# A fourth token tile between two embedding products, a root moved to GpSimd, and PSUM banks counted from 4

## The chip, the cores and the metric

One NeuronCore of a Trainium2 chip runs the whole program as one launch. The metric is the device time in microseconds (us) of an execution; the number given is the median of several runs.

## The reference

The input is x, 512 tokens of 1024 features in float32. The first half of the model has two layers, each a mixer, an MLP and an embedding gate. With LN the layer norm, it reads, cut to what matters here:

```python
for i in range(2):
    y = mixer_i(h)                                   # even: mLSTM + sparse attention; odd: latent attention
    h = _layer_norm(DN_ALPHA * h + y, ln1_g[i], ln1_b[i])
    u = jnp.square(jax.nn.relu(h @ mlp_w1[i])) @ mlp_w2[i]      # 1024 -> 4096 -> 1024
    h = _layer_norm(DN_ALPHA * h + u, ln2_g[i], ln2_b[i])
    h = h + jax.nn.sigmoid(h @ ple_gate_w[i]) * (p[i] @ ple_w[i])
```

The second half has two layers more. Each is a gated ffn, 1024 to 2816 and back, added by half; a hybrid mixer; and a second ffn. In front of each of the three stands a norm, `xf * rsqrt(mean(xf^2) + eps) * g`.

## The kernel before

**Tiles.** X holds the 512 tokens as four token tiles (j or m, 0 to 3) of 128 partitions by 1024 features. A product needs its input with the features on the partitions. So behind each norm TensorE turns every token tile: 8 transposes of 128x128 into two PSUM banks. ScalarE (ACT) copies these rounded ("hi") and VectorE (DVE) writes the difference ("lo") into `H`, which empties the banks. Weights are split the same way: ACT writes a hi half, DVE a lo half, into buffers used in turn. A product is three matmuls, hi*hi, hi*lo and lo*hi.

**Layers.** `lin(name, ...)` is one layer of 512 output columns. It goes through its weights in pieces of two k blocks, and in each piece through four output tiles m, 6 matmuls for each (p, m). Each m has a PSUM bank of its own, which is full after the last piece. Names: `up`/`dn` are the MLP's two products, `pw` is p @ ple_w (2 k blocks, one piece), `pg` the gate's product (8 k blocks, four pieces), `gu`/`fd` those of the ffns, `h` and `wo` those of the hybrid. Digits name the layer and the part: pg10 is the first half of pg of layer 1.

**Banks.** `bank(..., of=...)` takes the next of a pool, counted by `taken[of]`: "all" is banks 0 to 7, "lin" 0 to 3, "side" 4 to 7. TensorE waits until that bank has been emptied.

**Joins.** Where one block passes into the next through a norm, `joint` sets the order on TensorE. In the last layer of the block (`last`) the tiles m come one after another over all its tail pieces, so that token tile 0 is done first and can be normed while TensorE is at the next. `slots` {(m, x): [j]} says behind which piece x of which m token tile j is turned. The first layer of the next block can be done by halves (`first`): its first two pieces are multiplied for the tokens of tiles 0 and 1 (u=0) and then for tiles 2 and 3 (u=1), in matmuls of 256 columns. `mid` {(u, x): [j]} says ahead of which piece of which half a tile is turned. Ahead of a half's first piece TensorE waits until that half's tiles are emptied. The joins that the change touches: `lx20` and `lx21` (from dn031 and dn131 to pg00 and pg10, with the pw layers between; not by halves) and `fx10` (from pg11 to gu100, by halves). Layers done by halves are up000, up100, gu100, h00, gu200, gu110, h10 and gu210.

**Order on the engines.** Each engine's program is written out by hand and runs in order; evictions of a layer are handed on as `side` and woven between the splits of the next layer's weights. In lx20 and lx21 DVE does for each tile: add the product to X, statistics, a scaling, a reciprocal of ACT's root, a second scaling (`ln_scaled`), and then the subtraction for the tile before (`turned`). In fx10 the tile's path is ACT's Sigmoid, DVE's product and sum into X, ACT's Square with its sum in `r1`, ACT's Sqrt (`rms_root`), DVE's reciprocal and scaling (`rms_scaled`). `told` waits for a signal. GpSimd (POOL) does small parts of the mixers only.

Of the kernel before, what the change touches and what calls it, by code (L numbers as in the profile page):

```python
# [415 lines left out]
def tensor_program(e, K, S, lins):  # L416
# [56 lines left out]
    def close(L, p, m, i, ms):  # L473
        b, end = K.turn[L.name, m], p is L.pieces[-1]
        if m == ms[-1]:
            i.then_inc(S["used"], 1)
            if end:
                b.full = (S["used"], p.i + 1)
        elif end:
            full(b, i)  # L480

    def lin(name, src, ready=None, ms=range(4), mix=None, each=None, of=None, last=None, first=None):

        L, ps = lins[name], lins[name].pieces
        whole = slice(0, 512)
        of = of or ("lin" if last or first or mix is not None else "all")
        if first:
            for u in range(2):  # L490
                for x, p in enumerate(ps[0:2]):
                    first(u, x)
                    if u == 0:
                        e.wait_ge(S["lo"], p.i + 1)
                    for m in ms:
                        i = tile(L, p, m, src, slice(256 * u, 256 * u + 256), of)
                        if u:
                            close(L, p, m, i, ms)
        for p in ps[2 if first else 0:len(ps) - (L.tail if last else 0)]:
            e.wait_ge(S["lo"], p.i + 1)  # L500
            for m in ms:
                for kk in range(p.k, p.k + p.c):
                    for r in ready(kk) if ready and m == ms[0] else ():
                        e.wait_ge(*r)
                    if each and kk % 4 == 0:
                        e.wait_ge(*each(kk, m))
                close(L, p, m, tile(L, p, m, src, whole, of), ms)
                if mix is not None:
                    next(mix, None)
        if last:  # L510
            for m in ms:
                for x, p in enumerate(ps[-L.tail:]):
                    if m == ms[0]:
                        e.wait_ge(S["lo"], p.i + 1)
                    for kk in range(p.k, p.k + p.c):
                        for r in ready(kk) if ready and m == ms[0] else ():
                            e.wait_ge(*r)
                        if each and kk % 4 == 0:
                            e.wait_ge(*each(kk, m))
                    close(L, p, m, tile(L, p, m, src, whole, of), ms)  # L520
                    last(m, x)
# [28 lines left out]

    def rms_joint(name):
        n = JOINS.index(name)
        return joint(name, K.n.xn, lambda j: (S["xn"], 4 * n + j + 1), {(2, 0): [0], (3, 0): [1]}, {(0, 1): [2, 3]})

    def ln_joint(name, n):
        slots, mid = {"lx10": ({(2, 1): [0], (3, 1): [1]}, {(1, 0): [2, 3]}),
                      "lx11": ({(2, 0): [0], (3, 0): [1]}, {(0, 0): [2], (0, 1): [3]})}.get(name, ({(2, 1): [0], (3, 1): [1]}, {}))
        return joint(name, K.X, lambda j: (S["ln_x"], 4 * n + j + 1), slots, mid)

    def to_fm(name, src, nf, ready, of="all"):  # L560
# [195 lines left out]
    def mlp_ple(l, J):  # L756
        nonlocal ucount
        U, base = K.m.U, {}

        def up(p):  # L760
            nonlocal ucount
            base[p] = ucount
            for c in range(2):
                if p + c == 0:
                    lin(f"up{l}{p}{c}", H, J.ready, first=J.first)
                else:
                    lin(f"up{l}{p}{c}", H)
            ucount += 8
        up(0)
        J2 = ln_joint(f"lx2{l}", 2 * l + 1)  # L770
        for p in range(4):
            if p < 3:
                up(p + 1)
            for c in range(2):
                lin(f"dn{l}{p}{c}", U[p % 2], (lambda k: [(S["u"], base[p] + k + 1)]) if c == 0 else None,
                    of=("side", "lin")[c] if p == 3 else None, last=J2.last if p + c == 4 else None)
        for c in range(2):
            lin(f"pw{l}{c}", K.m.pT, (lambda k: [(S["pt"], 2 * l + k + 1)]) if c == 0 else None, of="lin")
            J2.turned(2 + c)
        J3 = rms_joint("fx10") if l else joint("ox", K.X, lambda j: (S["ple_x"], 5 + j), {(2, 0): [0], (3, 0): [1]}, {})  # L780
        lin(f"pg{l}0", H, each=J2.each, of="side")
        lin(f"pg{l}1", H, last=J3.last)
        return J3
# [360 lines left out]
def scalar_program(a, K, S, lins):  # L1144
# [322 lines left out]
            act(K.n.xn[:, m, 0:512], X[:, m, 0:512], ACT.Square, "jn_a" if m == 3 else None, accum_out=r0[:, m:m + 1])  # L1467
            yield

    def rms_root(j, added):  # L1470
        a.wait_ge(*added(j))
        act(K.n.xn[:, j, 0:512], X[:, j, 512:1024], ACT.Square, accum_out=r1[:, j:j + 1])
        if j == 0:
            told("jn_d")
        act(r1[:, j:j + 1], r1[:, j:j + 1], ACT.Sqrt, "jn_a", scale=1.0 / 1024, bias=r0[:, j:j + 1])

    def rms_join(name, then, added, gate=none):
        p = lins[then].pieces
        if name in ("fx10", "hx0", "fx11", "hx1"):
            split(p[0])  # L1480
            split(p[1])
            flush()
            for j in (0, 1):
                next(gate, None)
                rms_root(j, added)
            turned(name, 0)
            next(gate, None)
            turned(name, 1)
            rms_root(2, added)
            next(gate, None)  # L1490
            rms_root(3, added)
            turned(name, 2)
            turned(name, 3)
            return
        split(p[0])
        flush()
        next(gate, None)
        next(gate, None)
        rms_root(0, added)
        rms_root(1, added)  # L1500
        turned(name, 0)
        next(gate, None)
        next(gate, None)
        turned(name, 1, (0,))
        rms_root(2, added)
        turned(name, 1, (1,))
        rms_root(3, added)
        split(p[1])
        turned(name, 2)
        turned(name, 3)  # L1510

    def mlp_ple(l):
# [42 lines left out]
        turned(name, 0)  # L1555
        ln_root(2)
        turned(name, 1)
        ln_root(3)
        projected(0)
        turned(name, 2)  # L1560
        prime(f"pg{l}0")
        projected(1)
        turned(name, 3)

        def ev_gate(c):
            for m in range(4):
# [494 lines left out]
def vector_program(v, K, S, lins):  # L2061
# [196 lines left out]
            turned(name, j)  # L2258
        side = none

    def rms_scaled(j, ld, sig):
        if j == 0:
            v.wait_ge(S[f"ring{ld.slot}"], ld.landed)
        told("jn_a")
        recip(r1[:, j:j + 1], r1[:, j:j + 1])
        stt(K.n.xn[:, j, :], X[:, j, :], r1[:, j:j + 1], K.RING[:, ld.slot, 0:1024], ALU.mult, ALU.mult, sig)

    def half_summed():
# [3 lines left out]
    def rms_join(name, then):  # L2272
        nonlocal side
        p, ld = lins[then].pieces, lins["g" + name]
        split(p[0])
        if name in ("fx10", "hx0", "fx11", "hx1"):
            split(p[1])
            half_summed()
            for j in (0, 1):
                next(side)  # L2280
                rms_scaled(j, ld, "xn")
            turned(name, 0)
            next(side)
            turned(name, 1)
            rms_scaled(2, ld, "xn")
            next(side)
            rms_scaled(3, ld, "xn")
            turned(name, 2)
            turned(name, 3)
            side = none  # L2290
            return
        half_summed()
        next(side)
        rms_scaled(0, ld, "xn")
        next(side)
        rms_scaled(1, ld, "xn")
        turned(name, 0)
        next(side)
        next(side)
        turned(name, 1, (0,))  # L2300
        rms_scaled(2, ld, "xn")
        turned(name, 1, (1,))
        rms_scaled(3, ld, "xn")
        split(p[1])
        turned(name, 2)
        turned(name, 3)
        side = none
# [867 lines left out]
def pool_program(g, K, S, lins):  # L3175
# [5 lines left out]
    E = K.e  # L3181
# [47 lines left out]
    for x in range(24):  # L3229
# [11 lines left out]
            g.tensor_tensor(isc[:, w - 128:w], isc[:, w - 128:w], K.cst("cmask"), ALU.add).then_inc(S["isc"], 1)  # L3241
        if x == 7:
            rotation(3)
    for l in range(2):
        g.wait_ge(*K.turn[f"hx{l}", 3, 1].full)
        g.memset(K.y.GROW, 0.0).then_inc(S["pool"], 1)
# [36 lines left out]
def sync_program(s, K, S, W, loads):  # L3283
# [15 lines left out]
    for j in range(4):  # L3299
# [3 lines left out]

SIGNALS = ["id", "c", "c2", "x0", "x1", "x2", "x3", "pos", "act", "dve", "pool", "used", "hi", "lo", "to_act", "to_dve", "e_rows", "conv", "acv", "silu", "n_v", "e_ya", "e_yb", "aog",
           "ml_d", "ml_e", "ml_m", "ml_y", "ml_v", "ml_r", "ml_b", "ml_z", "power", "e_blk", "c_s", "c_e", "c_p", "n_m", "ln_x", "u", "pt", "ple_x", "cq", "lat", "qrope", "qirope",
           "ix_s", "ix_a", "isc", "gp", "madd", "a_m", "m_v", "od_a", "od_d", "xn", "jn_a", "jn_d", "hc", "cv", "hi_v", "hp_a", "hp_d", "rw_a", "rw_d", "hv_a", "hv_d", "gp_a", "gp_d", "lr_a", "lr_d", "lru", "grow", "h67", "st", "kd", "hd", "he", "xl",
           "oh", "sq", "bbr", "s0x", "s1", "kw", "xi", "xd", "gz", "gn_a", "gn_d", "ct", "state", "og_t", "og", "done", "out"]

def build(nc, ctx, W, lins, loads):
# [166 lines left out]
```

## Time and profile before

| what | value |
|---|---|
| median of 3 runs | 3831.24 us (3826.64 to 3834.88) |
| the profiled execution: its time, its span | 3827.86 us, 3825.9 us |
| TensorE (PE) busy | 3702.0 us, 97% of the span |
| VectorE (DVE) busy | 1884.6 us, 49% |
| ScalarE (ACT) busy | 1442.1 us, 38% |
| GpSimd (POOL) busy | 170.1 us, 4% |
| mean granted TensorE clock, of full speed | 0.989 |

Times in the rows are microseconds from the span's start. The end of a matmul is modelled, so a busy PE is not a PE at its peak, and some records of matmuls can be missing. What stands in brackets is how long the engine was idle ahead of the row, and which instruction's end released it. L445 and L454 are helpers (matmul, transpose), L1157 is ACT's helper `act`, L2081 to L2105 are DVE's.

### The profile page before, as it was taken

Reading aid. Unit: us, or ns where it says so; the run is one execution under the profiler, and the core shown is the slowest. Engines: PE = TensorE matmul, PEld = TensorE weight load, DVE = VectorE, ACT = ScalarE, POOL = GpSimd, SP = SyncE. Lnnn points to the kernel's source line nnn. Section 1 sums busy time; section 2 is a strip of 40 time slices with the busy share of each in tenths; the row PEclk is TensorE's granted clock in tenths of the full one; section 3 lists DMA queues with packets and bytes.
Section 4 is the critical chain, followed back from the end, with each engine's and each line's share of the span. In section 5 each row is a group of like instructions: output and inputs, shape, how many; then the busy total and the mean of one; then the engine's idle time right before and its main releaser. Section 6 shows DMA issues by size and latency. Waiting matters only on the chain.

```text
span 3825.9 us, 46047 instructions
## 1 busy us (share of the span) xinstructions
PE 3702.0 (97%) x18208; PEld 3016.8 (79%) x18208; DVE 1884.6 (49%) x2674; ACT 1442.1 (38%) x2178; POOL 170.1 (4%) x157
## 2 busy tenths in 40 slices
PE   9998899999999999999999999999999999999999
PEld 7776788887668887788877797888888877887887
DVE  4455644466755445433367564333433476563333
ACT  3344332336534322432255443322322354443322
POOL 0003000000100000000000220000000000400000
PEclk9999999999999999999999999999999999999999
DMA  4000222222003222222221012222222221012222
GB/s 177 34 34 34 77 97 92 98 89 93 19 34 121 100 94 93 99 96 93 92 90 58 12 62 88 99 90 92 100 99 99 72 101 47 33 41 99 99 89 72
DMA packets 45285, 306.91 MB, mean 80 GB/s; under 512 B 5136, under 2 KB 5520, under 8 KB 10640
## 3 DMA queue, kind: packets, MB, share of 16 engines
q1 hardware_dynamic: 45072, 303.97, 22.4%
q8 instruction: 145, 2.38, 0.3%
q14 instruction: 68, 0.56, 0.0%
HBM read 301.86 MB, written 2.10 MB: 79 GB/s over the span
## 4 chain that ended last, share of the span: by engine, by line
PE 82%; DVE 11%; ACT 5%; issue 1%; POOL 0%; DMA 0%; DVEq 0%; ACTq 0%; SPq 0%; POOLq 0%
PE ps L445 79%; DVE split L2081 3%; ACT arena L1157 3%; PE ps L454 2%; DVE arena L2081 2%; DVE arena L2085 2%; DVE X L2085 2%; ACT split L1157 2%; ACT L1157 1%; DVE arena L2928 1%; DVE small L2097 0%; DVE arena L2077 0%; DVE arena L2109 0%; DMA X<-in_x 0%; DVE arena L2089 0%
## 5 line engine op out<-in xcount | busy, mean ns | idle before, releaser
L445 PE MATMUL ps<-split 128*128 128x512 f32 (+2 forms) x13596 | 3099.0, 387 | 53.4 <-DVE split L2081 18.5
L445 PEld LDWEIGHTS ps<-split 128*128 128x128 f32 x13596 | 2486.4, 189 | 586.7 <-issue 53.4
L2081 DVE TENSOR_TENSOR split<-ring,split 128x1024 fp32r<-128x1024 f32 x554 | 675.2, 1219 | 1211.9 <-ACT split L1157 1193.7
L1157 ACT ACTIVATE split<-ring 128x1024 fp32r<-128x1024 f32 x554 | 583.0, 1052 | 1280.8 <-PE ps L445 1240.9
L445 PE MATMUL ps<-arena 128*128 128x128 f32 (+9 forms) x3344 | 493.1, 300 | 32.7 <-ACT arena L1157 10.4
L445 PEld LDWEIGHTS ps<-arena 128*128 128x128 f32 (+2 forms) x3344 | 399.9, 192 | 110.2 <-issue 76.8
L1157 ACT ACTIVATE arena<-ps 128x512 f32<-128x512 f32 (+6 forms) x580 | 297.9, 514 | 384.4 <-PE ps L445 213.4
L2081 DVE TENSOR_TENSOR arena<-arena 128x512 f32<-128x512 f32 (+5 forms) x254 | 150.5, 593 | 69.9 <-ACT split L1157 49.8
L1157 ACT ACTIVATE split<-arena 128x512 fp32r<-128x512 f32 x156 | 98.8, 634 | 164.7 <-DVE arena L2081 162.4
L2081 DVE TENSOR_TENSOR arena<-arena,ps 128x512 f32<-128x512 f32 x176 | 121.0, 688 | 40.9 <-PE ps L445 22.0
L2081 DVE TENSOR_TENSOR split<-arena,split 128x512 fp32r<-128x512 f32 x156 | 108.0, 692 | 64.2 <-ACT split L1157 61.6
L1157 ACT ACTIVATE arena<-arena 128x512 f32<-128x512 f32 (+9 forms) x141 | 103.7, 736 | 82.1 <-DVE arena L2085 22.0
L454 PE MATMUL ps<-C,arena 128*128 128x128 f32 (+4 forms) x764 | 116.4, 278 | 18.0 <-DVE arena L2085 12.9
L1157 ACT ACTIVATE arena<-ps,arena 128x128 f32<-128x128 f32 (+3 forms) x144 | 68.4, 475 | 156.8 <-DVE arena L2113 151.4
L2081 DVE TENSOR_TENSOR split<-ps,split 128x512 fp32r<-128x512 f32 x126 | 87.2, 692 | 77.2 <-ACT split L1157 66.9
L454 PEld LDWEIGHTS ps<-C,arena 128*128 128x128 f32 (+4 forms) x764 | 90.5, 145 | 40.4 <-DVE arena L2085 16.7
L2085 DVE SCALAR_TENSOR_TENSOR X<-ps,X 128x512 f32<-128x512 f32 x136 | 94.1, 692 | 53.9 <-PE ps L445 42.8
L1157 ACT ACTIVATE split<-ps 128x512 fp32r<-128x512 f32 x126 | 75.4, 598 | 67.9 <-PE ps L454 58.7
L2085 DVE SCALAR_TENSOR_TENSOR arena<-arena,C 128x511 f32<-128x511 f32 (+2 forms) x108 | 82.6, 765 | 23.7 <-ACT arena L1157 18.5
L1157 ACT ACT_TABLE_LOAD x70 | 89.8, 1283 | 6.8 <-DVE arena L2089 1.5
L2113 DVE TENSOR_REDUCE arena<-ps 128x1 f32<-128x128 f32 (+3 forms) x96 | 47.2, 492 | 90.0 <-PE ps L445 86.3
L2089 DVE COPY arena<-ps 128x256 f32<-128x256 f32 (+8 forms) x98 | 44.0, 449 | 95.8 <-PE ps L445 56.6
(98 smaller groups left out, 978.6 us busy)
## 6 DMA issues: line engine op xcount, KB each, us to landing
ring<-in_wts SPq DMA_DIRECT2D x268, 1024.0 KB, 4.8
ring<-in_wts SPq DMA_DIRECT2D x25, 512.0 KB, 3.4
X<-in_x SPq DMA_DIRECT2D x4, 512.0 KB, 5.8
out<-arena SPq DMA_DIRECT2D x4, 512.0 KB, 2.6
ring<-in_wts SPq DMA_DIRECT2D x2, 784.0 KB, 4.4
C<-in_cb SPq DMA_DIRECT2D x1, 1403.5 KB, 14.4
ring<-in_wts SPq DMA_DIRECT2D x2, 576.0 KB, 10.5
C<-in_cb SPq DMA_DIRECT2D x1, 512.0 KB, 6.3
```

Source lines behind the costliest of these rows:

```text
L445: return e.matmul(out, l, r, start=start, stop=stop, skip_group_check=True)
L454: return e.transpose(out, i, ident[0:k, 0:k])
L1157: o.sig(a.activation(out, i, f, **kw), sig)
L2081: o.sig(v.tensor_tensor(out, a, b, op), sig)
L2085: o.sig(v.scalar_tensor_tensor(out, a, s, b, o0, o1), sig)
L2089: o.sig(v.tensor_copy(out, i), sig)
L2113: o.sig(v.tensor_reduce(out, i, AX.X, op, negate=neg), sig)
L2928: o.sig(v.copy_predicated(Y.ST[h][:, 0:4, :], mk, by4(b.t[:, :])), b)
```

## The change

1. Behind a layer by halves the counter of the pool "all" is set to 4.
2. In lx20 and lx21 token tile 2 is turned behind the last piece of the last m of dn031 or dn131, where it was turned between pw0 and pw1; tile 3 is turned between pw0 and pw1, where it was turned behind pw1. ACT's order follows.
3. In fx10 tile 3 is turned ahead of the second half, where it was turned with tile 2 ahead of the first half's second piece. Its inverse root is made on GpSimd, by a tensor_scalar (mean and eps) and a power of -0.5, each on 128x1, where it was ACT's Sqrt and DVE's reciprocal.

```diff
@@ lin, end of "if first:"
+            taken["all"] = 4
@@ rms_joint
-        return joint(name, K.n.xn, ..., {(2, 0): [0], (3, 0): [1]}, {(0, 1): [2, 3]})
+        return joint(name, K.n.xn, ..., {(2, 0): [0], (3, 0): [1]}, {(0, 1): [2], (1, 0): [3]} if name == "fx10" else {(0, 1): [2, 3]})
@@ ln_joint, for lx20 and lx21
-                      ... .get(name, ({(2, 1): [0], (3, 1): [1]}, {}))
+                      ... .get(name, ({(2, 1): [0], (3, 1): [1], (3, 3): [2]}, {}))
@@ tensor_program, mlp_ple
             lin(f"pw{l}{c}", K.m.pT, ..., of="lin")
-            J2.turned(2 + c)
+            if c == 0:
+                J2.turned(3)
@@ scalar_program, rms_root (pooled is true for fx10)
+        if pooled:
+            if j == 0:
+                told("jn_d")
+            act(K.n.xn[:, j, 0:512], X[:, j, 512:1024], ACT.Square, "fx_s", accum_out=r1[:, j:j + 1])
+            return
@@ scalar_program, mlp_ple
         turned(name, 1)
+        turned(name, 2)
         ln_root(3)
         projected(0)
-        turned(name, 2)
+        turned(name, 3)
         prime(f"pg{l}0")
         projected(1)
-        turned(name, 3)
@@ vector_program, rms_scaled
-        told("jn_a")
-        recip(r1[:, j:j + 1], r1[:, j:j + 1])
+        if pooled:
+            v.wait_ge(S["fx_r"], j + 1)
+        else:
+            told("jn_a")
+            recip(r1[:, j:j + 1], r1[:, j:j + 1])
@@ pool_program, behind the index scores of the odd mixer, ahead of the hybrid's memset
+    r0, r1 = K.SM[:, 24:28], K.SM[:, 20:24]
+    for j in range(4):
+        g.wait_ge(S["fx_s"], j + 1)
+        g.tensor_scalar(r1[:, j:j + 1], r1[:, j:j + 1], 1.0 / 1024, r0[:, j:j + 1], ALU.mult, ALU.add).then_inc(S["fx_m"], 1)
+        g.wait_ge(S["fx_m"], j + 1)
+        g.tensor_tensor(r1[:, j:j + 1], r1[:, j:j + 1], E.power, ALU.pow).then_inc(S["fx_r"], 1)
```

## Rows read from the trace of the kernel before

**Rows 1.** of the page's part 1, TensorE: busy us (share), instructions
```profile
PE 3702.0 (97%) x18208; PEld 3016.8 (79%) x18208; DVE 1884.6 (49%) x2674; ACT 1442.1 (38%) x2178; POOL 170.1 (4%) x157
```

**Rows 2.** the chain that ended last: start, length, what
```profile
468.25 296.79 PE ps L445 x1308
...
1152.99 303.68 PE ps L445 x1368
```

**Rows 3.** timeline of PE: start, us, engine, line, tiles, count [idle before <-releaser]
```profile
468.25 12.08 PE L445 MATMUL ps<-split 128*128 128x512 f32 x52 [1.27 <-ACT arena L1157]
...
1577.39 21.82 PE L445 MATMUL ps<-split 128*128 128x256 f32 x126
...
1601.13 1.66 PE L445 MATMUL ps<-split 128*128 128x512 f32 x6 [1.92 <-DVE arena L2081]
...
2356.36 1.66 PE L445 MATMUL ps<-split 128*128 128x512 f32 x6 [0.56 <-DVE arena L2081]
2358.57 5.72 PE L445 MATMUL ps<-split 128*128 128x512 f32 x24 [0.55 <-DVE arena L2081]
...
3478.87 3.75 PE L445 MATMUL ps<-split 128*128 128x512 f32 x8 [5.58 <-DVE arena L2081]
```

**Rows 4.** timeline of all engines behind gu200
```profile
2354.26 1.23 DVE L2081 TENSOR_TENSOR split<-ring,split 128x1024 fp32r<-128x1024 f32 x1 [4.26 <-ACT split L1157]
2355.61 0.69 DVE L2081 TENSOR_TENSOR arena<-arena,ps 128x512 f32<-128x512 f32 x1
```

**Rows 5.** timeline of PE, at dn130 and fd1020
```profile
1459.90 4.37 PE L445 MATMUL ps<-split 128*128 128x512 f32 x18 [0.53 <-DVE X L2085]
...
1908.81 23.43 PE L445 MATMUL ps<-split 128*128 128x512 f32 x102 [0.54 <-DVE X L2085]
```

**Rows 6.** timeline of all engines in the join lx20 (PEld: weight loads)
```profile
789.67 8.45 PE L445 MATMUL ps<-split 128*128 128x512 f32 x36
...
791.16 1.28 DVE L2085 SCALAR_TENSOR_TENSOR X<-X,small,ring 128x1024 f32<-128x1024 f32 x1
...
797.62 1.28 DVE L2085 SCALAR_TENSOR_TENSOR X<-X,small,ring 128x1024 f32<-128x1024 f32 x1
...
798.73 5.30 PEld L445 LDWEIGHTS ps<-split 128*128 128x128 f32 x24
...
806.20 1.49 DVE L2081 TENSOR_TENSOR split<-ps,split 128x512 fp32r<-128x512 f32 x2 [4.99 <-ACT split L1157]
...
809.07 3.06 PEld L445 LDWEIGHTS ps<-split 128*128 128x128 f32 x8 [3.98 <-DVE split L2081]
```

**Rows 7.** timeline of PEld in the join lx21
```profile
1518.95 6.22 PEld L445 LDWEIGHTS ps<-split 128*128 128x128 f32 x17 [3.72 <-DVE split L2081]
```

**Rows 8.** timeline of all engines in the join fx10
```profile
1553.55 0.19 ACT L1157 ACTIVATION_READ_ACCUMULATOR arena<-X 128x1 f32 x1
1553.81 1.28 ACT L1157 ACT_TABLE_LOAD   x1
1555.11 0.30 ACT L1157 ACTIVATE small<-small 128x1 f32<-128x1 f32 x1
...
1555.69 1.28 DVE L2085 SCALAR_TENSOR_TENSOR arena<-X,small,ring 128x1024 f32<-128x1024 f32 x1
...
1557.03 1.09 PE L454 MATMUL ps<-C,arena 128*128 128x128 f32 x8 [1.29 <-DVE arena L2085]
...
1575.77 1.97 PE L454 MATMUL ps<-C,arena 128*128 128x128 f32 x8 [3.46 <-DVE arena L2085]
```

**Rows 9.** groups on POOL, shapes apart: busy us, mean ns
```profile
L3196 POOL TENSOR_SCALAR arena<-arena,small 128x512 f32<-128x512 f32 x4 | 8.0, 1997 | 314.7 <-PE ps L445 314.7
...
L3209 POOL TENSOR_TENSOR arena<-arena,small 128x4 f32<-128x4 f32 x4 | 4.1, 1032 | 21.9 <-DVE arena L2077 21.9
L3196 POOL TENSOR_SCALAR arena<-arena,small 128x128 f32<-128x128 f32 x4 | 2.9, 718 | 0.0
```

**Rows 10.** timeline of PE at the hybrid's first inverse
```profile
2188.59 8.28 PE L445 MATMUL ps<-arena 128*128 128x128 f32 x72 [1.00 <-ACT arena L1157]
```

More of the change, by code:

```diff
@@ L552, in rms_joint @@
         n = JOINS.index(name)
-        return joint(name, K.n.xn, lambda j: (S["xn"], 4 * n + j + 1), {(2, 0): [0], (3, 0): [1]}, {(0, 1): [2, 3]})
+        return joint(name, K.n.xn, lambda j: (S["xn"], 4 * n + j + 1), {(2, 0): [0], (3, 0): [1]}, {(0, 1): [2], (1, 0): [3]} if name == "fx10" else {(0, 1): [2, 3]})
     def ln_joint(name, n):
         slots, mid = {"lx10": ({(2, 1): [0], (3, 1): [1]}, {(1, 0): [2, 3]}),
-                      "lx11": ({(2, 0): [0], (3, 0): [1]}, {(0, 0): [2], (0, 1): [3]})}.get(name, ({(2, 1): [0], (3, 1): [1]}, {}))
+                      "lx11": ({(2, 0): [0], (3, 0): [1]}, {(0, 0): [2], (0, 1): [3]})}.get(name, ({(2, 1): [0], (3, 1): [1], (3, 3): [2]}, {}))
         return joint(name, K.X, lambda j: (S["ln_x"], 4 * n + j + 1), slots, mid)
@@ L1468, in half_squares, with rms_root @@
             yield
-    def rms_root(j, added):
+    def rms_root(j, added, pooled=False):
         a.wait_ge(*added(j))
+        if pooled:
[3 more added lines that the diff above has]
+            return
         act(K.n.xn[:, j, 0:512], X[:, j, 512:1024], ACT.Square, accum_out=r1[:, j:j + 1])
@@ L1482, in rms_join @@
             flush()
+            pooled = name == "fx10"
             for j in (0, 1):
                 next(gate, None)
-                rms_root(j, added)
+                rms_root(j, added, pooled)
             turned(name, 0)
@@ L1488, in rms_join @@
             turned(name, 1)
-            rms_root(2, added)
+            rms_root(2, added, pooled)
             next(gate, None)
-            rms_root(3, added)
+            rms_root(3, added, pooled)
             turned(name, 2)
@@ L2259, in ln_join, with rms_scaled @@
         side = none
-    def rms_scaled(j, ld, sig):
+    def rms_scaled(j, ld, sig, pooled=False):
         if j == 0:
             v.wait_ge(S[f"ring{ld.slot}"], ld.landed)
-        told("jn_a")
-        recip(r1[:, j:j + 1], r1[:, j:j + 1])
+        if pooled:
[3 more added lines that the diff above has]
+            recip(r1[:, j:j + 1], r1[:, j:j + 1])
         stt(K.n.xn[:, j, :], X[:, j, :], r1[:, j:j + 1], K.RING[:, ld.slot, 0:1024], ALU.mult, ALU.mult, sig)
@@ L2278, in rms_join @@
             half_summed()
+            pooled = name == "fx10"
             for j in (0, 1):
                 next(side)
-                rms_scaled(j, ld, "xn")
+                rms_scaled(j, ld, "xn", pooled)
             turned(name, 0)
@@ L2284, in rms_join @@
             turned(name, 1)
-            rms_scaled(2, ld, "xn")
+            rms_scaled(2, ld, "xn", pooled)
             next(side)
-            rms_scaled(3, ld, "xn")
+            rms_scaled(3, ld, "xn", pooled)
             turned(name, 2)
@@ L3305 @@
            "ml_d", "ml_e", "ml_m", "ml_y", "ml_v", "ml_r", "ml_b", "ml_z", "power", "e_blk", "c_s", "c_e", "c_p", "n_m", "ln_x", "u", "pt", "ple_x", "cq", "lat", "qrope", "qirope",
-           "ix_s", "ix_a", "isc", "gp", "madd", "a_m", "m_v", "od_a", "od_d", "xn", "jn_a", "jn_d", "hc", "cv", "hi_v", "hp_a", "hp_d", "rw_a", "rw_d", "hv_a", "hv_d", "gp_a", "gp_d", "lr_a", "lr_d", "lru", "grow", "h67", "st", "kd", "hd", "he", "xl",
+           "ix_s", "ix_a", "isc", "gp", "madd", "a_m", "m_v", "od_a", "od_d", "xn", "jn_a", "jn_d", "fx_s", "fx_m", "fx_r", "hc", "cv", "hi_v", "hp_a", "hp_d", "rw_a", "rw_d", "hv_a", "hv_d", "gp_a", "gp_d", "lr_a", "lr_d", "lru", "grow", "h67", "st", "kd", "hd", "he", "xl",
            "oh", "sq", "bbr", "s0x", "s1", "kw", "xi", "xd", "gz", "gn_a", "gn_d", "ct", "state", "og_t", "og", "done", "out"]
```

## The prediction

> **What bounds the kernel now.** I read the busy shares first: TensorE is busy 97% of the span, so nothing but its own idle stretches can be won [rows 1]. Then the chain that ended last: its long pieces are matmuls without a break, and what lies between them is the joins of two blocks (a norm, its transposes, the first product behind it) [rows 2]. So I read TensorE's timeline around each place that the diff touches, to see which wait ends last there. All numbers below are lost start time: of 6 matmuls from start to start, 2.21 us passed where 6 without a stall take 1.34 (24 weight loads in 5.30 and a gap of 0.03, [rows 6]), so an idle of 0.55 us in the PE rows means 0.87 us lost; the rest is the modelled end of a matmul [rows 3].
>
> **Part 1: banks counted from 4.** A layer by halves takes banks 0 to 3 ("lin"). The layer behind it counts in "all". I counted the calls of `bank` in the program: that counter stands at 0 (mod 8) behind up000, gu100, gu200, gu110 and gu210, so the next layer wants banks 0 to 3 again, still being emptied; behind up100 it stands at 4 already. The trace agrees: a stall at 468.25, 1601.13 and 2356.36/2358.57, and none behind up100, where the chain's piece runs 304 us from 1152.99 [rows 2, 3]. What ends the stall is the eviction of tiles 2 and 3 on VectorE, which stands behind the lo half of the next weights (1.23 us from 2354.26) in its queue [rows 4]. With banks 4 to 7, empty since the join, that eviction has 20 us more.
> - up001: idle 1.27, so 1.6 us.
> - gu201 has two stalls, 0.56 and 0.55: 0.87 each, 1.7. gu101 shows 1.92, but its block before has 126 matmuls where the code issues 132 (24 + 48 halves, 48 whole, 12 of the next layer): six missing records, 1.35 us; it is the same 1.7. So I read the 5.58 at 3478.87 too: missing records, not a long stall. Four such places: 7.0.
> - The other end: after an odd or even number of layers the last "all" layer stands in banks 0 to 3 or 4 to 7, and the next product (dn030, dn130, fd20, "side") takes 4 to 7. Each ffn has 14 such layers: from 0 they end in 4 to 7 and cost a stall of 0.54 [rows 5]; three more rows, at 2662.66, 3030.27 and 3789.26, repeat it; from 4 they end in 0 to 3 and it goes: 4 x 0.85 = 3.4. The MLP has 13: from 0 it ends in 0 to 3 (the chain's piece from 468.25 runs unbroken to 765), from 4 it ends in 4 to 7, as mlp 1 does now with a stall of 0.53. So mlp 0 gains one: -0.85.
> - In the hybrid the 72 "all" banks of the triangular inverses shift by four too. They follow each other as before; only the edge is new: vx of tile 0 takes the bank of c0 of tile 2. It waits for the eviction of v1 anyway, which ACT does after that of c0, and starts at 2188.59 [rows 10]. Nothing; cover gone, it would be one eviction, 0.6 us, per layer.
> Sum of part 1: 1.6 + 7.0 + 3.4 - 0.85 = 11.1 us.
>
> **Part 2: tiles 2 and 3 of lx20 and lx21.** Now: tile 1 turned, 12 matmuls of dn031, 24 of pw0, tile 2, 24 of pw1, tile 3, whose transposes end at 805.1, and then 4.0 us in which TensorE waits for the lo half of pg0's weights (809.07) [rows 6]. That lo half is late since VectorE's queue has tile 3's two subtractions ahead of it (806.20 to 807.7), which wait for ACT's copy; and tile 3 comes late only because pw1 stands before it: it was ready at 797.62 + 1.28 = 798.9. After: dn031 ends at 789.64 + 12 x 0.223 = 792.3; tile 2 is ready at 791.16 + 1.28 = 792.45, so about 0.2 of a new wait; its transposes take 1.0, pw0 5.4, to 799.0, just behind tile 3's 798.9; transposes to 800.0, pw1 to 805.4. Hidden work: ACT evicts pw0's last tile to 799.9, turns tile 3 to 801.2, splits pg0's two pieces to 803.4; VectorE's lo halves are done at 803.6 and 804.8. So pg0 starts at 805.4 in place of 809.07: 3.7 us. The order also puts ACT's copy of tile 2 ahead of the root of tile 3: the copy can end at 794.9, the root takes 0.2, and VectorE needs it by 797.4, just ahead of the scaling at 797.62, a margin of 2.3 us; behind that root hang tile 3, pg0 and VectorE's queue. No DMA moves: pg0's second half still waits for tile 3's `ln_x`, at the same time. lx21 repeats the pattern with an idle of 3.72 [rows 7]: 3.7. Sum of part 2: 7.4.
>
> **Part 3: the join fx10.** Now each tile's sum of squares is followed on ACT by a table load of 1.28, a root, and VectorE's reciprocal; and the next Sigmoid loads its table back. Seven loads, 9.0 us of ACT [rows 8]. From the end of the square's accumulation (1553.74) to VectorE's scaling (1555.69) it is 1.95 us. After, this path c is: signal 0.1, GpSimd's tensor_scalar on one column, signal 0.1, power on one column, signal 0.1. Neither column form is in the trace. Tensor_scalar took 0.72 for 128 columns and 2.00 for 512, a line that meets 0.29 at none: between 0.29 and 0.72, I take 0.3. Power took 1.03 for 4 columns [rows 9]: between 0.26 (a quarter of it) and 1.03 (all of it fixed); with tensor_scalar's fixed part of 0.29 of the row above, one column is 0.29 + 0.74/4, nearer the lower end: 0.4. So c = 1.0, at most 2.1. GpSimd has nothing else to do there: its queue stands behind the index scores, long done, and ahead of the hybrid's memset, which waits for hx0.
> Walked through VectorE's order with c = 1.0: tile 0 scaled at 1556.05, turned at 1556.1 (now 1557.03); tile 1's Sigmoid no longer waits for a load; m=3 of pg11 ends at 1567.2 for TensorE; Sigmoid, two VectorE operations of 0.7, square, c, scaling: tile 3 ready at 1572.8 (now 1575.7). Moving tile 3 behind the second piece of the first half: u=0 first piece to 1570.2, tile 2 to 1571.2, second piece (24 half-width, 3.0) to 1574.2, tile 3 to 1575.1. Here comes a new wait: the second half's tokens need tile 3 emptied, an ACT copy 0.6 and a VectorE subtraction 0.7 behind the transposes, to 1576.35; now the second piece hides it. The second half starts at 1576.35 in place of 1577.3 + 3.0 = 1580.3: 3.9 us. With c = 2.1 the delay enters twice (tiles 0 to 2 through VectorE's queue, tile 3 on its own): 2.1 us. I take 3.9.
> The Trainium skill, "ScalarE: Activation LUTs", section "What ACT_TABLE_LOAD costs", puts a switch at a load of about 1.28 and a drain of about 1.38. The load agrees with this trace; the drain does not show: the root starts 0.02 behind the load's end. By the page the seven switches would be 18.6 us of ACT instead of 9.0 and part 3 might be worth some 2 us more, as an estimate.
>
> **Sum.** 11.1 + 7.4 + 3.9 = 22.4, some 22 after the small new waits. Against the profiled execution (span 3825.9, time 3827.9) that is 3805.5. The profiled one lies 3.4 below the median of the runs, so: 3831.2 - 22.2 = 3809.0.
>
> **Rivals.**
> - GpSimd is slow (0.15): a first use that costs, or power on one column at the four-column price and more. The same queue's long waits are the place; c of 3.1 takes part 3 to nothing: 3813.
> - The bank stalls come back elsewhere (0.10): the freed layers run into the lo halves of their own weights. For: VectorE's split ends just ahead of the evictions [rows 4]. Against: two pieces, 10 us, of weights are ready ahead, and behind up100 no stall follows. It would leave half of part 1: 3814 to 3815.
> - Part 2 turned into a wait (0.08): tile 2 late by more than the 2.3 us margin, so that ACT holds tile 3's root back; it keeps half: 3812.7.
> - The 5.58 was a real stall (0.05): 4 us more, 3805 or less.
> - Slower (0.03): the shifted banks make each round of the inverses wait for the eviction of the round before. There are 24 rounds in each of two layers: 0.46 us a round eats the gain of 22, a full eviction of 0.6 us gives 3838. Against: the order among the 72 banks is unchanged.
> - TensorE's clock: no row ties it to these places.
>
> **From the cases to the numbers.** The forecast holds 0.59. The median itself moves (3826.6 to 3834.9), so its own range is 3804 to 3814. To leave out no more than 0.2 I reach to the weak cases above and to the 5.58 below: 3801 to 3818. A measurement tells about 0.2%, 7.7 us, from no change. Every rival but the slower one stays below 3823.6; two together, or unsteady runs, put 0.04 within: faster 0.93, same 0.05, slower 0.02.
>
> **What would show it.** In the profile after: no idle of TensorE behind the layers by halves but in fx10's join; none before fd20; a new 0.5 before dn030; pg0 starting straight behind pw1; GpSimd rows of [128x1], power near 0.4; two table loads at most in fx10, and an idle of 1.3 behind tile 3. Wrong would make me: power above 1.1 us, a wait for tile 2 of lx20 over 0.5, or waits inside the inverses.

## The result

| | before | after |
|---|---|---|
| median, range, runs | 3829.39 us, 3826.64 to 3834.88, 4 | 3791.73 us, 3789.87 to 3795.67, 4 |
| profiled execution: time, span | 3827.86, 3825.9 | 3795.67, 3793.9 |
| mean granted TensorE clock | 0.989 | 0.991 |

The ratio is 0.9901, 95% interval 0.9884 to 0.9918: 37.7 us faster (31 to 44). The forecast, 22 us and a range from 3801 to 3818, is missed on the fast side. The profiled execution of after is the slowest of its four, so profile against profile shows 32.0 us.

The page's first part, after. TensorE's busy time fell by 7.4 us while its instructions are the same [rows 1]. Some 2.7 of it is work that no longer runs at a low clock (the table on the whole span below); most of the rest is what the modelled ends of matmuls ahead of some 13 stalls make, 0.32 each, by an estimate from the 0.87 and 0.55 of the prediction.

```profile
PE 3694.6 (97%) x18208; PEld 3015.5 (79%) x18208; DVE 1885.9 (50%) x2670; ACT 1430.3 (38%) x2167; POOL 173.8 (5%) x165
```

The chain that ended last, after. Behind up000, gu200 and gu210, where the stalls of [rows 3] stood, the pieces now run on: 1344 matmuls from 447.74, and 1512 to 1608 from each layer by halves of an ffn to its next join, past fd20 as well.

```profile
447.74 299.79 PE ps L445 x1344
...
1565.36 337.87 PE ps L445 x1512
...
2314.20 340.78 PE ps L445 x1536
2679.53 340.51 PE ps L445 x1536
...
3430.42 357.10 PE ps L445 x1608
```

TensorE's timeline, after (start, us, count, idle before and what ended it). The forecast stall before dn030 is there (750.76). In lx20 pw1 and pg00 are one row from 800.99, where 3.98 was idle [rows 6]; lx21 is the same from 1505.11 [rows 7]. In fx10 the idles of 1.29 and 3.46 [rows 8] became 0.43 and, new behind tile 3, 1.07.

```profile
750.76 32.95 PE L445 MATMUL ps<-split 128*128 128x512 f32 x144 [0.53 <-DVE X L2093]
...
790.67 3.01 PE L445 MATMUL ps<-split 128*128 128x512 f32 x12
793.67 1.09 PE L454 MATMUL ps<-C,X 128*128 128x128 f32 x8
794.52 5.72 PE L445 MATMUL ps<-split 128*128 128x512 f32 x24
800.14 1.09 PE L454 MATMUL ps<-C,X 128*128 128x128 f32 x8
800.99 29.29 PE L445 MATMUL ps<-split 128*128 128x512 f32 x128
...
1505.11 39.70 PE L445 MATMUL ps<-split 128*128 128x512 f32 x174
1545.24 1.09 PE L454 MATMUL ps<-C,arena 128*128 128x128 f32 x8 [0.43 <-DVE arena L2093]
...
1565.36 35.03 PE L445 MATMUL ps<-split 128*128 128x256 f32 x176 [1.07 <-DVE split L2089]
```

All engines in fx10, after: from the end of the square's accumulation (1542.79) over the two GpSimd operations to DVE's scaling (1543.89) it is 1.10 us; the forecast had 1.0.

```profile
1542.60 0.19 ACT L1159 ACTIVATION_READ_ACCUMULATOR arena<-X 128x1 f32 x1
1542.90 0.26 POOL L3259 TENSOR_SCALAR small<-small 128x1 f32<-128x1 f32 x1 [554.60 <-ACT arena L1159]
1543.25 0.56 POOL L3261 TENSOR_TENSOR small<-small 128x1 f32<-128x1 f32 x1
...
1543.89 1.28 DVE L2093 SCALAR_TENSOR_TENSOR arena<-X,small,ring 128x1024 f32<-128x1024 f32 x1 [1.86 <-POOL small L3261]
```

So the forecast signs in the profile are there, but for power on one column, which took 0.56 and not 0.4, and yet 15 us more are gone. Two readings of the profile of before account for them.

**A stall taken for missing records.** All engines of before around gu101 and gu211. At 3478.87 TensorE had not run since 3473.3, and it starts right behind an eviction that ends at 3478.72. At gu101 two stalls end with two evictions, at 1601.08 and 1603.29.

```profile
1600.39 0.69 DVE L2081 TENSOR_TENSOR arena<-arena,ps 128x512 f32<-128x512 f32 x1
...
1602.60 0.69 DVE L2081 TENSOR_TENSOR arena<-arena,ps 128x512 f32<-128x512 f32 x1
...
3469.73 3.56 PE L445 MATMUL ps<-split 128*128 128x512 f32 x15
...
3475.82 0.69 DVE L2081 TENSOR_TENSOR arena<-arena,ps 128x512 f32<-128x512 f32 x1
...
3478.03 0.69 DVE L2081 TENSOR_TENSOR arena<-arena,ps 128x512 f32<-128x512 f32 x1
```

The counter of "all" does stand at 0 behind these layers, but I never asked where the pool "lin" stands. Most layers take four banks of it, which changes nothing; `qi` of the odd mixer takes three, and `hg` of each hybrid one, and these move it on. Counted through the program, tiles m0 to m3 lie in these banks: up000, gu200 and gu110 in 0, 1, 2, 3; gu100 in 3, 0, 1, 2; gu210 in 1, 2, 3, 0. The next layer's m0 wants bank 0. Behind gu200 that is m0's, long empty, and only m2 and m3 wait. Behind gu100 m1 and m2 wait for the evictions of m2 and m3, each one tile (6 matmuls) sooner. Behind gu210 m0 waits for the very last eviction. The "126 of 132" at 1577.39 [rows 3] is no loss of records: the stall comes ahead of m1, so 6 matmuls fewer stand before it.

**The clock behind a wait.** The windows of before (us, then each engine's busy time with its count; the third figure from the end is the granted clock): behind the wait of lx20 and behind the one at gu211, where it is near one half, the 1.2 GHz level of 2.4, before it is back at 1.00.

```profile
804.00:810.00 6.00, 2.26 (x12) 1.79 (x12) 3.49 (x4) 3.54 (x6) 0.00 (x0) 0.79 0.65 276
810.00:816.00 6.00, 6.00 (x19) 4.64 (x18) 1.57 (x2) 0.00 (x0) 0.00 (x0) 0.64 0.40 134
...
3472.00:3478.00 6.00, 1.29 (x6) 0.75 (x4) 2.60 (x3) 1.69 (x2) 0.00 (x0) 0.90 0.37 156
3478.00:3484.00 6.00, 5.13 (x13) 4.09 (x14) 1.38 (x2) 0.63 (x1) 0.00 (x0) 0.54 0.01 3
...
3486.00:3492.00 6.00, 6.00 (x28) 4.99 (x27) 1.23 (x1) 1.06 (x1) 0.00 (x0) 1.00 0.28 82
```

The window times one less the clock is 6 x 0.21 + 6 x 0.36 = 3.4 us at lx20 and 6 x 0.10 + 6 x 0.46 = 3.4 at gu211. That is more than what is lost, since the clock is low before the wait ends, and a low clock costs nothing while TensorE stands still: at gu211 it stands at 0.50 in a window in which no matmul runs.

```profile
3478.00:3478.50 0.50, 0.00 (x0) 0.00 (x0) 0.47 (x1) 0.00 (x0) 0.00 (x0) 0.50 0.00 0
```

Counted only where TensorE is busy, in windows of 0.5 us, the losses of this profile are 2.6 us at lx20, 2.7 at lx21, 1.6 at fx10 and 2.4 at gu211. The lengths of a row bear this out: the 150 matmuls behind the wait of lx21 took 36.79 us in before and 34.32 and 34.29 in the two runs with that wait filled (below), 2.5 less.

```profile
1518.95 36.79 PE L445 MATMUL ps<-split 128*128 128x512 f32 x150 [3.48 <-DVE split L2081]
...
1517.65 34.32 PE L445 MATMUL ps<-split 128*128 128x512 f32 x150 [0.36 <-DVE split L2084]
...
1514.91 34.29 PE L445 MATMUL ps<-split 128*128 128x512 f32 x150 [0.85 <-DVE split L2084]
```

At the same places after, the windows show 1.00:

```profile
798.00:804.00 6.00, 6.00 (x31) 4.87 (x31) 5.25 (x8) 4.64 (x8) 0.00 (x0) 1.00 0.48 160
804.00:810.00 6.00, 6.00 (x28) 4.95 (x28) 3.14 (x3) 4.04 (x6) 0.00 (x0) 1.00 1.00 415
...
3452.00:3458.00 6.00, 6.00 (x28) 4.96 (x27) 3.88 (x6) 2.32 (x3) 0.00 (x0) 1.00 0.00 0
```

The Trainium skill has the mechanism on the page "TensorE: Matmul & The Clock Gate", section "HAM oscillation — how this bites in real kernels": a wait in the matmul stream lets the clock fall, the work behind it starts at the low level, and half of that time is lost. The windows agree (0.54 behind the wait at gu211). Whether those falls hang on the waits, or happen anyway, was for the runs to say; the clock also falls in other places, differently in each execution.

### The profile page after: what moved, and what is told of

Read it like the earlier page. It is cut to its first block, busy times and chain, and to the rows that moved or that the text cites. A ratio compares the mean times of both kernels' runs of the same rounds, so it can differ in the third digit from the quotient of the medians.

```text
span 3793.9 us, 46039 instructions
## 1 busy us (share of the span) xinstructions
PE 3694.6 (97%) x18208; PEld 3015.5 (79%) x18208; DVE 1885.9 (50%) x2670; ACT 1430.3 (38%) x2167; POOL 173.8 (5%) x165
## 4 chain that ended last, share of the span: by engine, by line
PE 85%; DVE 9%; ACT 4%; issue 1%; POOL 1%; DMA 0%; DVEq 0%; ACTq 0%; SPq 0%
PE ps L445 82%; ACT arena L1159 2%; PE ps L454 2%; DVE split L2089 2%; DVE arena L2093 2%; DVE arena L2089 2%; DVE X L2093 1%; ACT split L1159 1%; DVE arena L2940 1%; ACT L1159 1%; DVE arena L2085 0%; DVE small L2105 0%; DVE arena L2117 0%; POOL arena L3208 0%; DMA X<-in_x 0%
## 5 line engine op out<-in xcount | busy, mean ns | idle before, releaser
L445 PE MATMUL ps<-split 128*128 128x512 f32 (+2 forms) x13596 | 3091.1, 387 | 32.7 <-DVE split L2089 12.3
L1159 ACT ACTIVATE arena<-arena 128x512 f32<-128x512 f32 (+9 forms) x141 | 103.5, 734 | 82.9 <-DVE arena L2093 22.4
L1159 ACT ACTIVATE split<-ps 128x512 fp32r<-128x512 f32 x126 | 75.4, 598 | 78.1 <-PE ps L454 69.6
```

The costliest lines, as they stand in the source:

```text
L445: return e.matmul(out, l, r, start=start, stop=stop, skip_group_check=True)
L1159: o.sig(a.activation(out, i, f, **kw), sig)
```

## The experiments

The theories: that only the waits themselves matter (W), and that each wait of some 3.5 us or more also costs a fall of the clock (C). C was priced before these runs at 1.7 or 3.4 us a fall, from whole windows, which is too much by what falls into the wait. For the banks: that my account of the missing records stands (M), or that the phase of "lin" sets the stall (P). In the diffs, + is what is added to the kernel before.

### Each part alone

Part 1 alone (3805.72 us; the kernel before beside it 3829.03):

```diff
@@ lin, end of "if first:"
+            taken["all"] = 4
```

> Part 1 alone: the counter of "all" set to 4, nothing else. Waits only (theory W): 11.1 us off, 0.9971. Waits and clock (theory C: a stall removed in a join also gives back the granted clock that fell behind it): the same 11.1, since the stalls of part 1 are 0.5 to 1.3 us and no fall of the clock stood behind them but one, at 3476 us of the profile of before; if that one belongs to the stall there, 14.5. The clock's falls behind lx20, lx21 and fx10 should still be there, 3.4, 3.4 and 1.7 us lost.

Measured: ratio 0.9944 (0.9930 to 0.9957), 21.4 us (16.5 to 27). The 11.1 forecast is outside, and so is 14.5, the same with one fall of the clock more. TensorE's timeline of this run: gu211 follows gu210 with no idle.

```profile
3439.88 40.43 PE L445 MATMUL ps<-split 128*128 128x256 f32 x211 [0.24 <-DVE split L2082]
```

Part 2 alone (3817.22 us):

```diff
@@ ln_joint, mid of lx20 and lx21
-({(2, 1): [0], (3, 1): [1]}, {})
+({(2, 1): [0], (3, 1): [1], (3, 3): [2]}, {})
@@ the loop over the pw layers
-            J2.turned(2 + c)
+            if c == 0:
+                J2.turned(3)
```

(ACT's order follows, as in the change.)

> Part 2 alone. W: 7.4 us off, two waits of 3.7, 0.9981. C: 7.4 and, as the fall of the granted clock behind each of the two waits goes, 2 x 3.4 more: 14.2, 0.9963; in its windows no fall behind pg00 and pg10 begins. A rival R, that the extra gain is scatter of the runs: 7.4, and falls of the clock at these two places as before.

Measured: 0.9973 (0.9961 to 0.9984), 10.3 us (6 to 15). The interval holds W's 7.4 and, just, C's 14.2; the middle is between them, near the 11.9 that C gives with the falls counted only where TensorE works (7.4 + 4.5, see the fillings). The clock at both places stays at 1.00.

Part 3 alone (3826.01 us), both halves of it:

```diff
@@ rms_joint (the place of tile 3)
-{(0, 1): [2, 3]}
+{(0, 1): [2], (1, 0): [3]} if name == "fx10" else {(0, 1): [2, 3]}
@@ rms_root, rms_scaled with pooled = name == "fx10" (the root), and on GpSimd
+    for j in range(4):
+        g.wait_ge(S["fx_s"], j + 1)
+        g.tensor_scalar(r1[:, j:j + 1], r1[:, j:j + 1], 1.0 / 1024, r0[:, j:j + 1], ALU.mult, ALU.add).then_inc(S["fx_m"], 1)
+        g.wait_ge(S["fx_m"], j + 1)
+        g.tensor_tensor(r1[:, j:j + 1], r1[:, j:j + 1], E.power, ALU.pow).then_inc(S["fx_r"], 1)
```

> Part 3 alone, both the root on GpSimd and the place of tile 3. W: 3.9 us off, 0.9990. C: 3.9 and 1.7 of clock: 5.6, 0.9985. lx20 and lx21 as before, with their falls of the clock.

Measured: 0.9989 (0.9981 to 0.9998), 4.2 us (1 to 7). W and C both fit. Together the three parts give 35.9, as the whole change does within its interval: they add up.

### Filling the waits of lx20 and lx21

The wait stays, but TensorE is kept at work in it. This adds work to the kernel before whose result nobody reads (first matmuls, then, in a second kernel, transposes):

```diff
@@ behind the second pw layer's J2.turned
+        e.wait_ge(*emptied(f"lx2{l}", 2, 0))
+        for f in range(14):
+            mm(K.turn[f"lx2{l}", 2, 0].t[...], K.X[:, 3, ...], K.X[:, 3, 0:128], True, True)
```

> The kernel before, and in the two waits of lx20 and lx21 TensorE does 14 matmuls of 128x128 in float32 into a bank that is free and overwritten afterwards (additional work, the result is unused). The waits stay: pg0 still waits for its lo half. W: 0 us. C: TensorE isn't idle, so the clock doesn't fall: 6.8 us off, 0.9982, and the windows behind the joins show full clock. If it takes longer than the wait of 4 us it costs the excess.

Measured: 3826.27 us, 0.9991 (0.9982 to 1.0000), 3.4 us faster (0 to 7) with more work done. TensorE's timeline (a float32 `mm` is two records) and windows: pg00 still waits, now 0.79 behind the filling, and the clock stays at 1.00 where it was 0.79 and 0.64.

```profile
804.95 1.04 PE L454 MATMUL ps<-C,X 128*128 128x128 f32 x8
805.82 3.29 PE L445 MATMUL ps<-X 128*128 128x128 f32 x28
809.90 10.31 PE L445 MATMUL ps<-split 128*128 128x512 f32 x44 [0.79 <-DVE split L2084]
```

```profile
804.00:810.00 6.00, 5.21 (x42) 4.77 (x40) 2.66 (x4) 4.28 (x7) 0.00 (x0) 1.00 0.82 345
810.00:816.00 6.00, 6.00 (x27) 4.92 (x28) 2.40 (x2) 0.28 (x1) 0.00 (x0) 1.00 0.42 134
```

```diff
@@ the same place, transposes in place of the matmuls (... stands for the columns, in both diffs)
+        for f in range(24):
+            tr(K.turn[f"lx2{l}", 2, 0].t[...], K.X[:, 3, ...])
```

> As the run with 14 matmuls in each of the two waits of lx20 and lx21, with 24 transposes of 128x128 in their place (additional work, the result is unused; 3.1 us each time). If only real matmuls keep the clock up, the falls behind pg00 and pg10 are there as in the kernel before and the time is 0 us off; if any activity of TensorE does, the falls are gone and the time is as with the matmuls, 3 to 7 us off.

Measured: 3821.16 us, against 3827.56 for before beside it, 0.9983 (0.9974 to 0.9992), 6.5 us faster (3 to 10). No fall at either place: transposes (the row's 32 are tile 3's 8 and these 24) hold the clock as matmuls do.

```profile
802.45 3.66 PE L454 MATMUL ps<-C,X 128*128 128x128 f32 x32
807.23 12.99 PE L445 MATMUL ps<-split 128*128 128x512 f32 x56 [1.12 <-DVE split L2084]
```

The Trainium skill says otherwise ("TensorE: Matmul & The Clock Gate", section "🔬 Part 4: PE-mode transpose": they do not count as busy for the clock in the same way); for these float32 transposes the measurement decides. From the start of tile 3's transposes to pg00's first matmul it is 4.77 us in before (804.30 to 809.07), 4.95 with the matmuls and 4.78 with the transposes, so the waits are as long as before and W gives nothing for either kernel. The transposes' interval leaves W out; that of the matmuls touches no change. In the seven profiles that keep both waits unfilled the falls cost 1.7 to 3.0 us each while TensorE works, in the mean 2.3, so 4.5 for both, which lies in both intervals.

### The counter behind gu210 alone

```diff
@@ lin, end of "if first:"
+            if name == "gu210":
+                taken["all"] = 4
```

> The kernel before with the counter of "all" set to 4 behind gu210 alone, one of the five places where it changes the bank. Theory M, that of the prediction (the idle of 5.58 us at 3478 is mostly missing records, a real stall of 1.7): 1.7 and 0.85 at the end of the ffn, 2.6 us off, 0.9993. Theory P (the phase of the pool "lin": gu210's tiles stand in banks 1, 2, 3, 0, so gu211's first tile wants the bank of gu210's last one; the idle is real, and the granted clock falls behind it): 5.9 + 0.85 + 3.4 = 10.1 us off, 0.9973, and no fall of the clock there in the windows.

Measured: 3821.92 us, 0.9977 (0.9968 to 0.9986), 8.8 us (5.4 to 12.2). M's 2.6 is outside, P's 10.1 inside (9.3 with the fall counted only where TensorE works, 2.5 in the mean of eight profiles). One row from gu210 on, no idle:

```profile
3449.03 51.31 PE L445 MATMUL ps<-split 128*128 128x256 f32 x259 [0.24 <-DVE split L2083]
```

### The halves of part 3

First only the place of tile 3 (the first hunk of the diff of part 3), with two idles of TensorE where the root is late and one behind tile 3:

> Of part 3 only the place of tile 3 in fx10 (ahead of the second half); the root stays on ACT. One look: the stretch from pg10's first matmul to the start of the second half of gu100. Tile 3 is ready at the same time as before, so the first half's second piece runs in the old wait of 3.5 us (3.0 us saved) but tile 3's eviction is no longer covered (1.3 us): 1.5 to 2 us shorter than in the kernel before at full clock. The wait is 0.5 to 1 us and another of 1.3 behind the transposes.

```profile
1558.02 1.09 PE L454 MATMUL ps<-C,arena 128*128 128x128 f32 x8 [1.27 <-DVE arena L2085]
...
1576.76 1.09 PE L454 MATMUL ps<-C,arena 128*128 128x128 f32 x8 [0.58 <-DVE arena L2085]
1579.24 18.25 PE L445 MATMUL ps<-split 128*128 128x256 f32 x102 [1.39 <-DVE split L2081]
```

Then only the root on GpSimd (the second hunk):

> Of part 3 only the root on GpSimd; tile 3 is turned with tile 2 as before. One look: tile 3 is ready about 3 us earlier, so the wait of 3.5 us ahead of its transposes is 0.3 to 1; the same stretch 3 us shorter at full clock, about as much as both edits together, and no fall of the clock behind it.

```profile
1554.83 1.09 PE L454 MATMUL ps<-C,arena 128*128 128x128 f32 x8 [0.43 <-DVE arena L2091]
...
1571.61 1.09 PE L454 MATMUL ps<-C,arena 128*128 128x128 f32 x8 [1.47 <-DVE arena L2091]
1572.46 21.14 PE L445 MATMUL ps<-split 128*128 128x256 f32 x126
```

The times are 3825.58 and 3822.49 (before there 3832.41, one run each, too few for differences of a few us). The timelines tell more. From pg10's first matmul to the first one behind the 1.92 us stall of gu101, with the time lost at a low clock taken off as above:

| kernel | from, to | us | lost at a low clock | left |
|---|---|---|---|---|
| before | 1518.95, 1601.13 | 82.2 | 4.3 | 77.9 |
| the order alone | 1519.81, 1599.41 | 79.6 | 2.8 | 76.8 |
| the root alone | 1518.44, 1595.52 | 77.1 | 1.7 | 75.4 |
| part 3, both | 1520.65, 1598.47 | 77.8 | 3.0 | 74.8 |

By waits the order alone is worth 1.1 (1.5 to 2 expected), the root alone 2.5 (3 expected; its wait ahead of tile 3's transposes is 1.47, not 0.3 to 1) and both 3.1. The two don't add up fully: with the root early the wait that the order fills is smaller.

### The two kernels again, and the last stall

The changed kernel once more, the kernel before once more, and the changed kernel with the counter of "all" moved by two banks twice in each MLP, ahead of its second and third up products, so that dn030 and dn130 find banks that are free:

> The changed kernel once more, beside the others of this call. Parts measured alone were 21.4, 10.4 and 4.2 us, 36.0 in sum: if they add up, 3793 and 0.9906. In the profile no fall of the clock behind pg00, pg10 or gu210.

> The kernel before, a second look. P: the idle of 5.58 us at about 3478, the idles of 4.0 and 3.7 behind pw01 and pw11 and that of 3.5 in fx10 are there to 0.1 us, and behind each the granted clock falls (1.7 or 3.4 us lost). If the falls are chance, one of the four at least has none.

```diff
@@ on top of the change, mlp_ple, top of its loop over p in range(4), ahead of up(p + 1)
+            if p < 2:
+                taken["all"] += 2
```

> The changed kernel, and in each MLP the counter of "all" is moved on by two banks twice, ahead of the second and the third up product, so that its 13 layers end in banks 0 to 3 and dn030 and dn130 find 4 to 7 empty. P: both stalls of 0.53 go, 2 x 0.85 = 1.7 us less than the changed kernel, which the runs can hardly tell and the profile can. A rival: the layers shifted by two meet banks that are not yet empty, then new stalls of 0.5 show behind up010, up110 and the layers two further.

The changed kernel: 3794.24 us, 0.9910 (0.9896 to 0.9923), 33 us, again below the range; its profile's span is 3788.9. The kernel before: 3829.82, with the same idles (5.57 at 3480.72) and all four falls of the clock. The third: 3791.88 us, 0.9906 (0.9892 to 0.9919). It beats the kernel before, but isn't told apart from the changed kernel. Its chain shows both stalls of 0.53 gone, as one piece in each MLP:

```profile
443.58 336.64 PE ps L445 x1500
...
1144.37 339.27 PE ps L445 x1524
```

**The falls of the clock over all profiles** (from windows of 2 and 0.5 us):

| wait | profiles with it | falls there, and us lost while TensorE works | profiles without it, or filled | falls there |
|---|---|---|---|---|
| lx20 and lx21, 4.0 and 3.7 us | 7 | both places in all 7, 1.7 to 3.0 each | 6 | none |
| gu211, 5.6 us | 8 | all 8, 2.3 to 2.9 | 5 | none |
| fx10, 3.5 us | 7 | 6, 1.4 to 1.7 each | 6 | none |
| gu101, 1.92 and 0.55 us | 9 | 2 (3.1 with the matmuls filled in, 1.6 with the order alone) | 4 | none |
| ahead of gu200, in the join, 2.0 us | 13 | 8, 1.7 each | 0 | |
| ahead of gu210, in the join, 2.0 us | 13 | 3, 1.7 each | 0 | |

So short waits aren't free of it: those near 2.0 us have a fall with them in 13 of 35 cases, those of some 3.5 us and more in 28 of 29. In before a fall stands behind a wait of 2.43 (ending at 915.64) and one of 2.50 (1151.61) too; places like these aren't in the table. Two of the falls at short waits, each with its row and its window: in before, in the join to gu200, and in the run with matmuls filled in, at gu101.

```profile
2318.70 1.12 PE L454 MATMUL ps<-C,arena 128*128 128x128 f32 x8 [2.02 <-DVE arena L2085]
2318.00:2324.00 6.00, 5.30 (x21) 4.31 (x22) 4.43 (x7) 2.21 (x5) 0.00 (x0) 0.72 0.01 3
...
1597.23 1.68 PE L445 MATMUL ps<-split 128*128 128x512 f32 x6 [1.92 <-DVE arena L2084]
1598.00:1604.00 6.00, 5.46 (x15) 3.96 (x14) 1.95 (x3) 0.63 (x1) 0.00 (x0) 0.56 0.01 3
```

**The whole span without the clock.** The same sum over each whole profile, taken from its span, leaves the time by waits and work alone:

| kernel | span, us | lost at a low clock | left |
|---|---|---|---|
| before | 3825.9, 3827.8 | 35.4, 39.7 | 3790.4, 3788.2 |
| waits filled with matmuls, with transposes | 3824.9, 3819.1 | 36.5, 29.5 | 3788.4, 3789.7 |
| part 1; part 2; part 3 | 3803.3; 3812.7; 3824.2 | 30.1; 29.9; 40.4 | 3773.2; 3782.8; 3783.8 |
| the counter behind gu210 alone | 3812.5 | 29.8 | 3782.6 |
| the change | 3793.9, 3788.9 | 32.7, 27.2 | 3761.2, 3761.7 |

The four kernels with all their waits agree within 2.2 us: the fillings changed nothing but the clock. The change is 27.8 us below before by waits, and parts 1 to 3 are 16.1, 6.5 and 5.5 below it, each to some 1 or 2 us. By the clock the two profiles of after lost 2.7 to 12.5 us less than the two of before. The falls at the places of the change go in both, but others come and go from one execution to the next.

## Why the prediction was wrong

- **"its block before has 126 matmuls where the code issues 132", "it is the same 1.7", "So I read the 5.58 at 3478.87 too: missing records, not a long stall".** This step failed. gu101 lost 2.2 + 0.87, 3.1 in place of 1.7; gu211 lost 5.9 in place of 1.7. Part 1's waits are 1.6 + 3.1 + 1.7 + 1.7 + 5.9 + 3.4 - 0.85 = 16.5, not 11.1. "The 5.58 was a real stall" stood as a rival with 0.05, priced well (4 us more) and weighed wrongly: the phase of "lin" was countable from the code, and DVE's eviction ending 0.15 ahead of the restart was in the trace.
- **"TensorE's clock: no row ties it to these places."** This step failed too, since windows around the waits had not been read. Counted while TensorE works, the falls removed are 2.5 at gu211, some 4.5 at lx20 and lx21 and 1.6 at fx10: 8.6 us. That they hang on the waits is shown at lx20 and lx21 by the two fillings, in which only the idle was filled; for gu211 and fx10 it rests on the table above. Part 1 also takes away the fall that gu101's stall has at times.
- **Part 1, the rest.** Right by the timelines: up001's stall, those at gu201 and gu111, and the four at the other end of the ffns went; the new one before dn030 came with 0.53; the first inverse of the hybrid follows an idle of 1.00 as before [rows 10].
- **Part 2.** 7.4 us by waits was right. From the first matmul of dn031's 12 to pg00's first it took 19.40 us (789.67 to 809.07 [rows 6]); now 790.67 to 800.99 and 24 matmuls of 0.223, 15.67: 3.7 less. The margin of 2.3 us held.
- **Part 3.** Sized 3.9, it measured 3.1 by waits; c was 1.10, not 1.0 (power 0.55, forecast 0.4; tensor_scalar 0.26, forecast 0.3). The wait behind tile 3 was forecast as 1.3 and shows as 1.07. The 0.8 that are missing I can't place on one row, and the whole span gives 5.5 for this part, so its size is known to 1 or 2 us only. The run's 4.2 holds a fall of the clock of 1.6 as well. The drain behind each table load that the Trainium skill has ("ScalarE: Activation LUTs", section "What ACT_TABLE_LOAD costs") would have made part 3 larger than forecast; on the stretch of this join it came out smaller.
- **Sum.** 16.5 + 7.4 + 3.1 = 27.0 by waits (the whole span gives 27.8) and 8.6 by the clock make 35.6, against 37.7 (31 to 44) and, run again, 33. The "22.4" was short by 5.4 in part 1 and by all of the clock, and 0.8 over in part 3. No rival on the slow side occurred.

Open: why a fall lasts about twice as long in one execution as in the next at the same wait; why one profile (part 2 alone) shows none behind fx10's 3.44, and why waits near 2.0 us have one only at times; and where part 3's 0.8 us are. These weren't tried.

## What to carry to other kernels

An idle that looks too long for its pattern is to be taken for a real wait until the engine that released it says otherwise: find the eviction that ended last and count which pool's bank it was, in both pools, since the phase of a rotating pool decides whether the next layer waits for a tile that is long done or for the last one. Price a TensorE wait of a few microseconds with the granted clock in the windows behind it, not by its length alone; here that added some 40 to 80 per cent. If such a wait can't be removed, harmless matmuls or transposes put in it can win back the part that the clock takes: in two waits of 4 us they won 3.4 us (0 to 7) and 6.5 (3 to 10). Count a low clock only where TensorE works.

## What the runs showed of the hardware

- At TensorE waits of 3.5 to 5.6 us the granted clock fell to half in 28 of 29 cases, in part before the wait had ended, and took 1.4 to 3.0 us more. At waits of 1.92 to 2.03 us it did so in 13 of 35 cases, and took 1.6 to 3.1.
- 28 records of 128x128 float32 matmuls (3.29 us) or 24 float32 transposes in the wait held the clock at full.
- GpSimd on one column: tensor_scalar 0.264 us, power 0.554 us (mean of 4 each), with 0.1 us from the end of one to the start of the next across a signal. Power on 4 columns took 1.03 in one profile and 1.23 in the other.
